# Two of the four prompt tiles through all 16384 experts as dense products, the other tiles by gathered rows

## The reference, cut to what matters

```python
q = (xf @ p['peer_wq']).reshape(n, PEER_HEADS, 2, PEER_HALF)
s1 = einsum('nhd,hkd->nhk', q[:, :, 0], p['peer_k1'])        # 8 heads x 128 keys
s2 = einsum('nhd,hkd->nhk', q[:, :, 1], p['peer_k2'])
v1, i1 = top_k(s1, 16); v2, i2 = top_k(s2, 16)
cand = v1[..., :, None] + v2[..., None, :]                   # 16 x 16 candidates
sc, sel = top_k(cand, 16)                                    # 16 experts per head
idx = i1 * 128 + i2 of the selected; gate = softmax(sc)
h = einsum('nhkd,nd->nhk', peer_u[idx], x)                   # 128 rows of U per token
a = gelu(h) * gate
out = einsum('nhk,nhkd->nd', a, peer_v[idx])                 # 128 rows of V per token
x2 = layer_norm(ALPHA * x1 + out)
```

## Time and profile before

| | us |
|---|---|
| median of 2 runs | 2170.19 (2167.76 to 2172.62) |
| profiled execution, span from first to last instruction | 2184.3 |
| TensorE busy | 1589.4 (73%) |
| VectorE busy | 1416.4 (65%) |
| GpSimd busy | 1345.5 (62%) |
| ScalarE busy | 386.9 (18%) |
| DMA | 675.05 MB, mean 309 GB/s |

### The profile page before, as it was taken

One profiled execution on the slowest core, in us unless ns is written; L12 is line 12 of the kernel. 1 busy time (PEld: TensorE's weight loads), 2 busy tenths in 40 slices (PEclk: granted clock), 3 DMA queues, 4 the chain that ended last, 5 costly groups with the idle time before them and its releaser, 6 DMA issues.

```text
span 2184.3 us, 16272 instructions
## 1 busy us (share of the span) xinstructions
PE 1589.4 (73%) x4705; PEld 801.6 (37%) x4705; DVE 1416.4 (65%) x3118; ACT 386.9 (18%) x905; POOL 1345.5 (62%) x1370
## 2 busy tenths in 40 slices
PE   6979976677887687776678667649567676677766
PEld 4667753344444333322233223213223232222222
DVE  7641257978998699768895677644567665444444
ACT  1222111222322122100211111111112121111111
POOL 0163004546666665677677777757777777777664
PEclk9979987877998888898889879869888888999999
DMA  5243345867999987999899999989999999999987
GB/s 219 86 94 95 135 154 206 328 219 257 350 355 346 377 311 261 382 359 338 306 368 365 374 353 381 363 311 357 377 364 344 355 375 375 379 357 387 373 334 293
DMA packets 186552, 675.05 MB, mean 309 GB/s; under 512 B 20960, under 2 KB 23440, under 8 KB 186048
## 3 DMA queue, kind: packets, MB, share of 16 engines
q0 software_dynamic: 167056, 609.25, 74.8%
q1 hardware_dynamic: 17632, 59.51, 7.6%
q10 hardware_dynamic: 1776, 5.24, 0.6%
HBM read 669.71 MB, written 3.69 MB: 308 GB/s over the span
## 4 chain that ended last, share of the span: by engine, by line
PE 27%; POOL 20%; DVE 18%; issue 16%; DMA 11%; another core or an unknown queue 4%; ACT 2%; ACTq 0%; SPq 0%; DVEq 0%; POOLq 0%
PE bank L795 13%; POOL region L507 7%; POOL region L500 6%; DMA region<-in_pv,region 5%; POOL wring L500 4%; PE bank L726 4%; DMA region<-in_pu,region 3%; DVE region L1195 3%; DVE region L1185 2%; PE bank L639 2%; POOL small L507 1%; PE bank L547 1%; PE bank L747 1%; POOL wring L507 1%
## 5 line engine op out<-in xcount | busy, mean ns | idle before, releaser
L795 PE MATMUL bank<-region,small 128*128 128x512 f32 (+1 forms) x1296 | 660.4, 658 | 309.5 <-ACT small L1439 130.6
L500 POOL DMA_INDIRECT region<-in_pu,region x348 | 392.6, 1128 | 313.7 <-DVE region L1195 122.6
L1195 DVE CUSTOM_DVE_ANT_0 region<-region 128x1024 f32<-128x1024 f32 x348 | 422.4, 1224 | 194.8 <-DMA region<-in_pu,region 163.7
L507 POOL DMA_INDIRECT region<-in_pv,region x392 | 438.4, 1118 | 167.0 <-issue 105.3
L795 PEld LDWEIGHTS bank<-region,small 128*128 128x128 f32 (+1 forms) x1296 | 253.8, 204 | 698.9 <-issue 563.7
L1195 DVE CUSTOM_DVE_ANT_0 wring<-wring,region 128x1024 f32<-128x1024 f32 x228 | 276.1, 1224 | 217.1 <-DMA wring<-in_pu,region 178.4
L500 POOL DMA_INDIRECT wring<-in_pu,region x228 | 239.2, 1049 | 69.5 <-issue 67.6
L1439 ACT ACTIVATE small<-small,region 128x128 f32<-128x128 f32 (+1 forms) x480 | 157.1, 387 | 701.2 <-DVE region L1169 284.6
L795 PE MATMUL bank<-discretisation,small 128*128 128x512 f32 (+1 forms) x196 | 114.3, 711 | 113.7 <-issue 62.8
L795 PE MATMUL bank<-wring,small 128*128 128x512 f32 x256 | 125.1, 622 | 28.1 <-issue 15.8
L726 PE MATMUL bank<-xT,wring 128*128 128x192 f32 (+1 forms) x512 | 131.0, 417 | 0.0
(11 more groups left out here) (242 smaller groups left out, 1720.5 us busy)
## 6 DMA issues: line engine op xcount, KB each, us to landing
wring<-in_w SPq DMA_DIRECT2D x104, 512.0 KB, 6.7
region<-in_pv,region POOLq DMA_INDIRECT x392
region<-in_pu,region POOLq DMA_INDIRECT x348
wring<-in_pu,region POOLq DMA_INDIRECT x228
out_y<-region ACTq DMA_DIRECT2D x4, 512.0 KB
small<-in_small ACTq DMA_DIRECT2D x1, 1669.0 KB, 14.0
xT<-in_xT SPq DMA_DIRECT2D x1, 1536.0 KB, 20.0
region<-in_x SPq DMA_DIRECT2D x3, 512.0 KB
```

The source lines that it names most:

```text
L500: pool.indirect_dma_start(ring_u[u_at.place[q]], None, io["pu"], bass.IndirectOffsetOnAxis(ind[:, k:k + 1], 0)).then_inc(g_u[u_at.place[q] ...
L507: pool.indirect_dma_start(ring_v[v_at.place[q]], None, io["pv"], bass.IndirectOffsetOnAxis(ind[:, k:k + 1], 0)).then_inc(g_v[v_at.place[q] ...
L795: last = mm(bank[6 + hf][0:tn, :], diag[:, d % DIAGS, 0:tn], ring_v[v_at.place[q]][:, 512 * hf:512 * hf + 512], start=k == 0, stop=t not i ...
L1195: V.tensor_tensor_reduce(out=ring_u[u_at.place[q]], in0=ring_u[u_at.place[q]], in1=x1[t], scale=1.0, scalar=0.0, op0=ALU.mult, op1=ALU.add ...
```

## The change

Tiles 3 and 4 no longer gather. `GATHER = [1, 0, 2]`, `DENSE = [3, 4]`. Selections are made in the order 1, 3, 4, 0, 2. The list has two parts after the first selection.

**First part.** The mixer of group 1, the rest of tile 1's selection, the whole selections of tiles 3 and 4, and for these two tiles the gate matrices, with the 128 slots of tile 1 spread between the items in proportion to `SPAN`. For a dense tile the high parts (i1), low parts (i2) and gates of each token's 128 choices are transposed (`gt`). Then, for four tokens at a time (`g`, 32 items a tile), VectorE makes for each token a 128 x 128 matrix with the gate where the row's i1 equals the column, ScalarE makes a one-hot matrix of i2 (`Abs`, then `Relu`), and TensorE multiplies the two: the result is the token's gates over all 16384 experts, as 128 x 128. ScalarE copies it into `stage` and stores blocks of 32 tokens, 2 MB each, to an internal tensor in HBM, `gates_by_chunk`. The first four `gates` items of group 1 are moved up among the attention products (`AHEAD`).

**Second part, the dense loop.** 128 chunks of 128 experts. SyncE streams 128 rows of U and 128 of V (512 KB each) through four slots of `wring`, and loads the gates of eight chunks at a time (1 MB). For each chunk TensorE transposes the U rows (`tr`, eight transposes, ScalarE copies them out), multiplies them with `xT` of the 256 dense tokens (`h`, eight products of 256 columns), ScalarE applies Gelu, VectorE multiplies with the gates, and TensorE multiplies with the V rows (`v`, four products of 512 columns) and accumulates over all chunks in banks 0 to 3. Beside it run the selections of tiles 0 and 2 (one item a chunk, chunks 0 to 19) and the 192 slots of these tiles (from chunk 12 to 122), all of whose V rows VectorE adds into `acc`.

**Slots.** A slot item is one slot, not four; Gelu, gate product, diagonal and adding follow 5, 6, 7 and 8 slots behind the dot. In the first part VectorE adds every second row of slots 0 to 95 and TensorE weighs all others. The rings are four places for U and five for V throughout.

```diff
-U_PLACES = ([0, 1, 2, 3, 4, 5], [0, 1, 2, 3], [0, 1, 2, 3] + list(range(6, 12)))
-V_PLACES = ([0, 1, 2, 3, 4, 5, 6, 7, 8], [0, 1, 2, 3, 4, 5], [0, 1, 2, 3, 4, 5] + list(range(9, 15)))
+GATHER, DENSE = [1, 0, 2], [3, 4]
+SELECT = [1, 3, 4, 0, 2]
+DT, D0 = 128 * len(DENSE), 320
+CHUNKS = NE // 128
+ACT_LAG, GATE_LAG, DIAG_LAG, ADD_LAG = 5, 6, 7, 8
+HOTS, BLOCK, GROUP = 4, 32, 8
+U_RING, V_RING = 4, 5
+TABLE_SLOTS = [1, 3, 5, 7]
+SPAN = {"qkv": 11, "turn": 2, "s": 9, "pv": 4, "gates": 10, "merge": 8, "wo": 14, "xt": 1, "wq": 5, "sc": 1, "top": 5, "choose": 9,
+        "gt": 1, "g": 2, "fold": 1}
...
+def weighed_by_vector(q):
+    return q >= 96 + 32 or (q < 96 and q % 2 == 1)
...
+    for t in DENSE:
+        some = selection(t)
+        for n, entry in enumerate(some):
+            take = -(-len(hots) // (len(some) - n))
+            entry += hots[:take]
+            hots = hots[take:]
+        mix += some
+        hots = [("g", t, i) for i in range(128 // HOTS)] if t in DENSE else []
+    mix += [hots[i:i + 2] for i in range(0, len(hots), 2)]
+    pre, q, at = 128, 0, 0
+    total = sum(SPAN[item[0]] for entry in mix for item in entry)
+    for entry in mix:
+        while q < pre and q * total <= at * pre:
+            s.append(("slot", q))
+            q += 1
+        s += entry
+        at += sum(SPAN[item[0]] for item in entry)
+    s += [("slot", n) for n in range(q, pre)] + [("lag", n) for n in range(pre, pre + ADD_LAG)] + [("close",), ("final", 1)]
+    s += [("tr", 0, 0), ("tr", 0, 1), ("tr", 1, 0), ("h", 0), ("tr", 1, 1)]
+    q, end, late = pre, NQ + ADD_LAG, selection(0) + selection(2)
+    for c in range(CHUNKS):
+        s += [("tr", c + 2, 0)] if c + 2 < CHUNKS else []
+        s += [("h", c + 1)] if c + 1 < CHUNKS else []
+        if late:
+            s += late.pop(0)
+        while q < end and (q - pre) * (CHUNKS - 6 - 12) <= (c - 12) * (end - pre):
+            s.append(("slot" if q >= pre + ADD_LAG else "dot", q))
+            q += 1
...
+        s += [("tr", c + 2, 1)] if c + 2 < CHUNKS else []
+        s.append(("v", c))
...
 @block.sync
+                if p[0] in ("du", "dv"):
+                    c = p[1]
+                    sp.dma_start(wring[:, slot_of[p], :], io["pu" if p[0] == "du" else "pv"][128 * c:128 * c + 128, :]).then_inc(w_here[slot_of[p]], 16)
...
+                if i == len(plan.pieces) + len(TABLE_SLOTS) - 1:
+                    for k in range(2):
+                        sp.wait_ge(g_out[k], 16 * (DT // BLOCK // 2))
+                    load_gates(sp, 0)
+                    load_gates(sp, 1)
...
 @block.gpsimd
+                    if q + U_RING < NQ and what != "lag" and not q < 128 <= q + U_RING:
+                        u_row(q + U_RING)
+                    if due(what, q - V_LAG):
+                        v_row(q - V_LAG)
...
 @block.tensor
+            def do_g(t, i):
+                n = DENSE.index(t) * (128 // HOTS) + i
+                pe.wait_ge(low_s, n + 1)
+                pe.wait_ge(high_s, HOTS * (n + 1))
+                b = enter(("g", t, i))
+                for k in range(HOTS):
+                    last = mm(b[:, 128 * k:128 * k + 128], low_hot[n % 2][:, k, :], high_hot[n % 2][:, k, :], start=True, stop=True)
+                last.then_inc(filled, 1)
+            def do_tr(c, hf):
+                b = enter(("tr", c, hf))
+                w = arrived("du", c)
+                for i in range(4):
+                    k = 4 * hf + i
+                    last = tr(b[:, 128 * i:128 * i + 128], w[:, 128 * k:128 * k + 128], ident)
+                last.then_inc(filled, 1)
+            def do_h(c):
+                b = enter(("h", c))
+                after(("tr", c, 1))
+                for k in range(KT):
+                    last = mm(b[:, 0:DT], UT[c % 2][:, k, :], xT[:, k, D0:TOK], start=k == 0, stop=k == KT - 1)
+                last.then_inc(filled, 1)
+            def do_v(c):
+                w = arrived("dv", c)
+                pe.wait_ge(dense_s, c + 1)
+                for j, t in enumerate(DENSE):
+                    for hf in range(2):
+                        b = enter(("va", t, hf)) if c == 0 else bank[2 * j + hf]
+                        last = mm(b[:, :], A[c % 2][:, 128 * j:128 * j + 128], w[:, 512 * hf:512 * hf + 512], start=c == 0, stop=c == CHUNKS - 1)
+                last.then_inc(filled, 1)
...
 @block.vector
+            def do_g(t, i):
...
+                for k in range(HOTS):
+                    at = HOTS * i + k
+                    V.tensor_scalar(high_hot[n % 2][:, k, :], iota, high[:, at:at + 1], gate[:, at:at + 1], ALU.is_equal, ALU.mult).then_inc(high_s, 1)
+            def do_h(c):
+                if c >= 2:
+                    dve.wait_ge(filled, plan.filled[("v", c - 2)])
+                g = c // GROUP
+                dve.wait_ge(g_in[g % 2], 16 * (g // 2 + 1))
+                dve.wait_ge(drained["A"], plan.drained[("h", c)][1])
+                V.tensor_tensor(of(A[c % 2]), of(hg[c % 2]), gates[g % 2][:, :, c % GROUP, :], ALU.mult).then_inc(dense_s, 1)
...
 @block.scalar
+            def low_hots(t, i):
...
+                for k in range(HOTS):
+                    last = S.activation(low_hot[n % 2][:, k, :], iota, ACT.Abs, bias=low[:, HOTS * i + k:HOTS * i + k + 1], scale=-1.0)
+                step(last)
+                S.activation(low_hot[n % 2], low_hot[n % 2], ACT.Relu, bias=1.0, scale=-1.0).then_inc(low_s, 1)
...
+                drain(("g", t, i), copy(stage[blk % 2].rearrange("p c t -> p t c")[:, part:part + HOTS, :], b[:, :].rearrange("p (t c) -> p t c", t=HOTS)))
+                if part + HOTS == BLOCK:
+                    act.dma_start(gates_out[blk], stage[blk % 2]).then_inc(g_out[blk % 2], 16)
+            def do_tr(c, hf):
+                b = full(("tr", c, hf))
+                drain(("tr", c, hf), copy(UT[c % 2][:, 4 * hf:4 * hf + 4, :], b[:, :].rearrange("p (k n) -> p k n", k=4)))
+            def do_h(c):
+                if c >= 2:
+                    act.wait_ge(dense_s, c - 1)
+                b = full(("h", c))
+                drain(("h", c), S.activation(hg[c % 2], b[:, 0:DT], ACT.Gelu))
```

More of the change, by code:

```diff
@@ L55, in n_slots, with tile_of, due @@
     return 64 if t == 0 else 128
+def tile_of(q):
+    return 1 if q < 128 else 0 if q < 192 else 2
+def weighed_by_vector(q):
+    return q >= 96 + 32 or (q < 96 and q % 2 == 1)
+def due(what, q):
+    return 0 <= q < NQ and (what == "slot" or (q < 128) == (what == "lag"))
 def schedule():
@@ L110, in schedule @@
-    s.append(("final", ORDER[-1]))
-    return s
-def mixer_first(items):
-    out, held = [], None
-    for item in items:
-        if item[0] in ("peer", "last") and held:
-            out.append(held)
-            held = None
-        if item[0] == "peer":
-            held = item
-            out.append(("before", *item[1:]))
-        else:
-            out.append(item)
-    return out + ([held] if held else [])
+    mix = [(first.pop(0) if first else []) + entry for entry in mix]
+    hots = []
@@ L130, in item_jobs @@
+    assert q == end and not late
+    return s + [("final", t) for t in DENSE]
 def item_jobs(item):
@@ new lines, in do_slot, with do_lag, do_dot, do_gt @@
+            def do_slot(q):
+                slot_work("slot", q)
+            def do_lag(q):
+                slot_work("lag", q)
+            def do_dot(q):
+                slot_work("dot", q)
+            def do_gt(t):
+                b = full(("gt", t))
+                if t == DENSE[0]:
+                    wait_item(act, ("wq", 0, 7))
+                if t - 2 in DENSE:
+                    act.wait_ge(filled, plan.filled[("g", t - 2, 128 // HOTS - 1)])
+                drain(("gt", t), copy(turned[t % 2], b[:, 0:384].rearrange("p (a n) -> p a n", a=3)))
```

518 lines of the change are left out of this document (282 added, 236 removed).

## The result

| | before | changed | ratio, 95% interval |
|---|---|---|---|
| first measurement | 2170.19 us (2167.76 to 2172.62) | 2327.29 us (2326.40 to 2328.18) | 1.0705, 1.0624 to 1.0787 |
| again, on the chip of the control below | 2175.88 us (2168.81 to 2183.41) | 2324.60 us (2323.81 to 2324.84) | 1.0671, 1.0648 to 1.0693 |

The changed kernel is 7% slower. The forecast was 2261 us, with 2120 to 2365 as range: the side was right, and the loss of 157 us is 1.7 times the forecast's 91.

A forecast was written before the change was run, and what follows sets the result against it. It took DMA to bound the old kernel's last part and VectorE its middle. 348 before gathers + 777 stage 1 + 1081 loop + 17 tail = 2223, plus 52 loss = 2275, less 14 span over median: 2261 us, range 2120 to 2365.

The forecast's parts named there:

- The loop, 1081 us: Dense loop: 106 chunks at 8.44 us and 22 at 8.0, 1071, plus 10 for VectorE in chunks 12 to 19.
- its half of the loss: Stage 1 and loop: 2.8% added, 52 us, half the 5.6% by which the old middle part exceeded its VectorE sum.
- 3.09 MB per chunk at 366 GB/s is 8.44 us: Dense loop, chunks with slots: DMA sets the pace, at the rate of the old kernel's long gather stretches.
- The rival without a DMA limit: Dense loop: memory gives over 386 GB/s, every chunk takes TensorE's 8.0 us; total 2162, with loss 2213; 25%.
- Stage 1, 777 us: Everything from 348 us to the dense loop: mixer, selections of tiles 3 and 4, one-hots, 128 slots, handover; 777 us.
- (f): Stage 1, tile 4's selection with tile 3's 32 one-hot groups and 25 slots: VectorE sum 143 us, 135 to 167.
- (g): Stage 1, tile 4's 32 one-hot groups with 13 slots: ScalarE, 89 us, or 108 if the strided copy costs double.
- (h): Stage 1, handover to the loop: last 2 MB of gates out, 1 MB in again, plus landings, 16 us.
- (a) to (e): Stage 1 through tile 3's selection: 79 to tile 1's choice, 120 attention, 122 merges and gates, 112 output and queries, 96 selection.
- Short rings: Rival, loop: with 4 and 5 ring places, late rows make a slot 5.3 us and a chunk 9.6; total 2336; 13%.
- The clock: Rival, loop: small waits keep TensorE's clock at 0.86, a chunk takes 9.3 us; total 2328; 8%.
- Seams that close: Faster rival: engines overlap across stage 1's pieces, 47 us less there, chunks at 8.0; total 2115; 12%.

The follow-up runs named there:

- the control: The changed kernel, unedited, run again beside the kernel before: 2324.60 us, ratio 1.0671.
- the queue is mended: Changed kernel with its gate loads cut in four behind successive U loads (2269.96 us), or left whole but issued from ScalarE's queue (2270.37 us).
- the spread kernel: Changed kernel with each 1 MB gate load cut into four of 256 KB, one behind each of four successive U loads: 2269.96 us.
- the one without transposes: Changed kernel with gate loads cut in four and U read in an order needing no transposes or ScalarE copies of them: 2215.40 us, ratio 1.0162.
- the kernel with the other queue: Changed kernel with the loop's 1 MB gate loads whole but issued from ScalarE's queue instead of SyncE's: 2270.37 us.
- two experiments: Changed kernel with gate loads cut into four of 256 KB, 2269.96 us; changed kernel with them whole from ScalarE's queue, 2270.37 us.
- the early start: Changed kernel with tile 1's norm and output behind the loop's first five items and the folded tile's copies 11 chunks later: 2309.45 us.
- Without slots there: Changed kernel with all 128 slots of tile 1 beside the mixer, none beside selections and one-hots of tiles 3 and 4: 2397.02 us.
- the run with all together: Changed kernel with split gate loads, earlier loop start, no transposes, low one-hots shared with VectorE, and tile 1 closed before the last ten groups: 2193.72 us, ratio 1.0383.

## Why the prediction was right in side and short in size

*The comparison that decides was right.* 256 slots at 3.06 us are 783 us; the dense work that takes their place has a floor of 993 us on TensorE, in which the other 192 slots (588 us at their old pace) cost 20 us once the queue is mended. Had the way from the first gather to the loop stayed at 637 us instead of 862, the change would by this sum have won (2325 - 225 = 2100 against a span of 2184). The forecast had 162 us more in front of the loop (348 + 799 against 985) and 71 less from there on (1111 + 17 against 1199), and that is what came, on both sides larger: +229 and -89.

*348 us before the first gather* and *17 us of tail*: the first gather is issued at 352.5, and 19 us follow the last V product's end.

*The chunk on TensorE, 8.0 us.* Measured 7.76. Two thirds of the difference are the transposes: four in 0.43 to 0.44 us from start to start, not 0.52 as in the earlier trace rows.

*The loop, 1081 us, 1111 with its half of the loss.* Measured 1092, to the end of the last V product. The size came out by luck; **the step "3.09 MB per chunk at 366 GB/s is 8.44 us" failed**. The 366 of the earlier trace rows is read from a stretch in which gathers alone fill the DMA engines (share 0.97). With nearly four tenths of the bytes streamed the spread kernel moves 398 GB/s over 360 us, and the one without transposes 400 over 760 us. The chip does not make the difference: the kernel with the other queue moves 398 too, where the kernel before took 2183 us. Whether the kind of transfer or the rings make it was not separated, and the earlier trace rows have 411 with gathers alone for 22 us. What filled most of the gap between 993 and 1091 was something that the forecast did not have at all: the gate load ahead of the table loads in SyncE's queue (36 us of waits and some 18 of half clock, both gone in two experiments) and ScalarE's program order (28 us in the loop; of its 38 with the handover the early start took 12). The rival without a DMA limit gave 1034 for the loop, and the spread kernel's is 1035: its mechanism, TensorE's chunk as the pace, was the true one, with DMA at 398 of some 400 GB/s close behind, and a second cost hid it. That the two numbers agree is chance: 993 us and 42 of waits and gaps against 1024 and 10. The Trainium skill (DMA: Bandwidth & Descriptors, Where 436 GB/s comes from) gives about 358 GB/s a core, half of what a memory stack delivers to two cores, as what binds such transfers. This kernel runs on one core, and these runs show 400 for 760 microseconds, so the measurement decides against it here.

*Stage 1, 777 us, 799 with its half of the loss.* Measured 862. This is where the size was lost, in three terms: **(f), (g) and (h) were priced too low, 248 us for a measured 315**, and the loss of 2.8% covers 7 of these 67.
(a) to (e) were 529; measured 547 from the first gather, and the loss of 2.8% covers 15 of the 18.
(f) was 143, measured 164. A 128x128 one-hot on VectorE stood for 0.25; it is 0.26 start to start (1.12 for four), so the term was right. But (f) was summed as if VectorE were always busy: it idles 28 of the 164 us, 10.7 of them for ScalarE in the slots' chain and 9.9 for one-hot products. Without slots there it is at 86 of 102, again with 11.9 us for one-hot products. These waits on the in-order chain are what the forecast did not price; up to 5 of the 21 us are the strided copy's, as (f) got shorter by that without the stride.
(g) was 89, measured 110. The forecast had the strided copy at 0.59 with 108 as the bound "if double". It is 1.05 to 1.06: the bound was the truth. Without the stride the products of the last 32 groups take some 14 of the 21 us less. The Trainium skill (SBUF — State Buffer, Door 1: The DMA port swizzle) notes that accesses which each go to a new 16-byte line of SBUF are slower, so that four float32 are as far as one may stride for free. The write here strides 32 of them, and the trace agrees, 1.06 against 0.58; by that note the forecast should have stood at its bound.
(h) was 16, measured 41. The forecast looked at DMA (gates out and in again) and there it is hidden; what decides is on the timeline of TensorE:

```profile
1172.54 8.63 PE L866 MATMUL bank<-region,small 128*128 128x512 f32 x16
1181.00 1.88 PE L866 MATMUL bank<-small 128*128 128x512 f32 x4
1183.73 5.39 PE L866 MATMUL bank<-region,small 128*128 128x512 f32 x12 [0.85 <-DMA region<-in_pv,region]
1188.96 1.88 PE L880 MATMUL bank<-region,small 128*128 128x512 f32 x4
1190.67 0.60 PE L904 MATMUL bank<-small,wring 128*128 128x128 f32 x4
1198.40 1.11 PE L904 MATMUL bank<-small,wring 128*128 128x128 f32 x4 [7.13 <-ACT region L1409]
1200.27 1.11 PE L904 MATMUL bank<-small,wring 128*128 128x128 f32 x4 [0.75 <-ACT region L1409]
```

From 1172.54 to 1190.67 it weighs the last eight rows of V and closes the sum, then it waits 7.13 us for ScalarE, whose next instruction in order is the root of tile 1's norm; the early start took 5 us of it. That the forecast's 16 were not wrong as a path, only not the longest, the run with all together shows: there the last one-hot product starts at 1162, tile 1 is long closed, and VectorE waits for the gates until 1177.

*The margin.* The span was taken to be 14 us over the median of the runs, as in the profiled execution before. After, the median is 2.7 over the span. That is 17 us of the miss that no mechanism stands behind.
In sum: 63 us in stage 1 (862 against 799), -19 in the loop (1092 against 1111), 6 before and after them, 17 of margin: 66 to 67 us, 2327 against 2261. With the loop at the pace of TensorE's chunk, as it truly runs, the forecast would have been the rival's 2213 and 114 us short: the wrong rate stood in for waits that it had not seen.

*The other rivals.* Short rings: in the loop VectorE waited 3.5 us in all for rows of U, far from 5.3 us a slot, so that is dead. The clock: 0.94 in the loop's first 206 us and 0.96 to 0.98 after them, not 0.86. Seams that close: stage 1 would have had to be under 742.

*The signs.* The first dense product was to come at about 1125; it came at 1214. Neither sign of an error on the high side appeared (no dots short of rows, no clock under 0.9), though the miss was on that side: the forecast had no sign for waits of one queue or for a handover that TensorE's own work fills.

## What to carry to other kernels

A rate read from one mix of transfers need not bound another: 366 GB/s of gathered rows were 398 to 400 in a loop that streamed nearly four tenths of its bytes, and what made the difference stays open. When work goes into a new loop with one full engine, list for each queue what stands in front of the load that this engine needs next; a large periodic load of another kind wants a queue of its own, or pieces small enough to stand between the others. And price the way into the new form (tables, one-hots, handovers) with each operation's layout, since it is serial: here leaving it out won 131 us, where the control is 149 slower than the kernel before.

## What the runs showed of the hardware

- A ScalarE copy of 128x512 from PSUM takes 1.06 us if it writes with a stride of 32 elements and 0.58 us if contiguous.
- A 1 MB load in pieces of 1 KB made the next 512 KB load of its queue be there only 17.6 us after its issue (changed kernel, at 1650.58); from another queue it cost no wait.
- The DMA engines carried 400 GB/s over 760 us, rows of 4 KB and gate pieces of 1 KB mixed, with 406 or 407 in eleven of twelve slices of the page and none above; TensorE was busy for only 703 of the 760 us in that run, the one without transposes.
- The kernel before, bound by gathers, differs by 3% between chips (2110 and 2176 us); the changed kernel's first 1214 us are the same on three chips within 2 us. Why the gathers differ was not traced.
